# A shared SBUF area moved from an odd multiple of 64 bytes to a multiple of 128, in a two-layer hybrid decoder trunk

## The chip, the cores and the metric

The kernel runs on one core of a Trainium2 chip. Its time is the device time of one execution in microseconds (us). Before the change it was 2750.69 us, the median of 3 runs (2748.47 to 2755.46).

## What is computed

The reference applies two decoder layers and a final RMSNorm to x of 1024 tokens by 1024 features, all in float32:

```
h = rmsnorm(x, norm_mix);  z = h @ w_in          # 1024 x 3336
y_ret  = retention(rq, rk, rv, rg)               # 6 heads of 64, chunks of 128 tokens
y_pool = pool_mix(pu)                            # trailing windows of 2, 4, 8, 16
y_ml   = mlstm(mq, mk, mv, mo, mi, mf)           # 4 heads of 96, chunks of 128 tokens
x = x + concat(y_ret, y_pool, y_ml) @ w_out
h = rmsnorm(x, norm_ffn);  gu = h @ w_gate_up    # 1024 x 5632
x = x + (silu(gu[:, :2816]) * gu[:, 2816:]) @ w_down
x = x + sigmoid(rmsnorm(x, norm_ple) @ w_ple_gate) * (p_i @ w_ple_proj)
```

## The kernel before, in words

Activations lie transposed in SBUF: features on the 128 partitions, in 8 groups (KC), and the 1024 tokens along the row, in two halves of 512.

**Three passes.** The large products are made in fp32r. Each float32 operand is split into a high part, rounded to fp32r, and a low part, the rest. A product is then high x high, low weight x high, and high weight x low activation, three matmuls of 128x512 into the same PSUM bank. `three_passes` (L1748 to L1753) issues them for the projections, the output projection, the first FFN tiles, the down projection and the gates; `product_of` (L1817 to L1830) does so for the FFN blocks. Each matmul has its own weight load. Twenty pairs of gate and up tiles per layer go through `block_products` (L1832), a scheme of seven products of half size in place of eight, of which four use sums of weights made by GpSimd (L1713). TensorE's other matmuls are float32: transposes, the chunk scores and states of the two mixers, the rotary permutation (L2034) and the centring of values (L2053).

**Order of the work.** One list, written out by `macro_schedule` (L85), is walked by each engine's program: norm, projection units, the chunk loop of the mLSTM with projection halves in between, the retention pairs with projection halves in between, the output projection, the FFN, and the per-layer embedding. Each engine waits on semaphores for what it needs.

**Who does what.** SP issues the loads of the weights in a fixed order (L1659 to L1670) into `w_raw` (two slots) and, in the FFN blocks, also into `turns`. GpSimd splits a weight tile into `w_hi` and `w_lo` (L1698, L1702), a ring of three tiles; for the FFN blocks ScalarE makes the high part (L1322) and GpSimd the low one (L1709). VectorE empties PSUM (L663, L1005), makes the low parts of activations (L560, L1012, L1077) and does most of the mixers' arithmetic. ScalarE makes the high parts of activations, the functions, and issues the DMAs of activations, which go to HBM and back between the FFN's two halves.

**Where things lie.** `build` allocates these tensors one after another, each start rounded up to 32 bytes; the numbers are bytes in a partition: `w_raw` at 1152, `w_hi` at 9344, `w_lo` at 21632, `const` at 33920, `par`, `early`, `rstd` at 45216, `turns` at 49312, `rows` at 57504, `small` at 65696, `zero1` at 65952 (4 bytes). Then comes the shared area, which `arena_at` (L272) and the allocation `arena` (L273) set, at 65984. The tensors in it are placed by hand with `at` (L276) and overlap in time. From its start: `h_hi`, `h_lo`, `x` and `mix` of 32768 bytes each, and from `w_at` 30720 bytes for what a stage needs. In `x`'s place lie `ml_qk` and `ret_qkv` for a time, in `mix`'s place `ffn_b` and `ple_in`, in `h_lo`'s `h_whole`, and behind `w_at` `ml_v`, `conv_raw`, `ml_kw`, `ml_c`, `ml_cols` (at 20032), `ml_so` (at 20672), `ml_vx`, `ml_km`, `ret_t`, `ffn_bw`, `p_hi`, `p_lo`, `ple_sig`, `squares`, `silu_g`, `square_sum`, `act`, `diag` and `w_sum`. The rows of an activation, 512 tokens of 4 bytes, begin at multiples of 2048 bytes from the area's start. `stat` and `tmp16` (L337, L338) are allocated behind it, `stat` at 227840.

```
WB = 30720
arena_at = -(-nc.sbuf_base // 64) * 64
sb("arena", [P, (4 * XB + WB + 64) // 4])
hh_at, hl_at, x_at, mix_at, w_at = [arena_at + i * XB for i in range(5)]
...
def three_passes(out, slot, col, rhi, rlo, first, final):
    wh, wl = whi[:, slot, col:col + P], wlo[:, slot, col:col + P]
    pe.matmul(out, wh, rhi, start=first, stop=False)
    pe.matmul(out, wl, rhi, start=False, stop=False)
    return pe.matmul(out, wh, rlo, start=False, stop=final)
```

Of the kernel before, what the change touches and what calls it, by code (L numbers as in the profile page):

```python
# [14 lines left out]
P = 128  # L15
# [227 lines left out]
def build(nc, w_d, x_d, p_d, pos_d, const_d, par_d, early_d, out_d):  # L243
# [3 lines left out]
    with ExitStack() as ctx:  # L247
        def sb(name, shape, dt=F32):
            return ctx.enter_context(nc.sbuf_tensor(name, shape, dt))[:]
# [19 lines left out]
        zero1 = sb("zero1", [P, 1])  # L269
        XB = 4 * KC * S  # L270
        WB = 30720
        arena_at = -(-nc.sbuf_base // 64) * 64  # L272
        sb("arena", [P, (4 * XB + WB + 64) // 4])  # L273
        hh_at, hl_at, x_at, mix_at, w_at = [arena_at + i * XB for i in range(5)]

        def at(name, offset, shape, dt=F32):  # L276
# [2026 lines left out]
```

## Time and profile before

| | |
|---|---|
| median of 3 runs | 2750.69 us |
| profiled execution | 2751.61 us |
| its span, first to last instruction | 2749.8 us |
| mean granted TensorE clock | 0.978 of full |
| TensorE busy | 2622.8 us, 95% |
| VectorE busy | 1506.1 us, 55% |
| GpSimd busy | 1284.3 us, 47% |
| ScalarE busy | 712.8 us, 26% |
| moved by DMA | 192.06 MB, 70 GB/s |

The span is divided among the engines by busy time, which overlaps from engine to engine. A matmul's duration runs until its result is out, so matmuls that follow one another overlap in the records, and their rate is read from their starts. A float32 matmul stands as two instructions in the records. A name such as h_hi<-x,par lists what is written and what is read; for a matmul the moving operand comes first and the weights second. PE, PEld, DVE, ACT and POOL are TensorE's matmuls, its weight loads, VectorE, ScalarE and GpSimd.

### The profile page before, as it was taken

To read this page: it belongs to the slowest core of one execution; us is meant where nothing else is said; L and a number is where in the kernel's file an instruction comes from. 1 tells how busy PE (TensorE), PEld (TensorE's weight loads), DVE (VectorE), ACT (ScalarE), POOL (GpSimd) and SP (SyncE) were. 2 spreads that over 40 slices of the span, in tenths; PEclk is the share of its full clock that TensorE was granted. 3 is DMA by queue.
4 is the path that set the end of the run, shared out by engine and by line. 5 is a ranking of instruction groups with operands and counts; after the bars stand their busy time and mean duration, and the time that the engine had idled before them with its cause. 6 is when DMAs were issued, how large, how long until landed. Compare 5 with 4: busy or idle time off the path is not lost.

```text
span 2749.8 us, 30657 instructions
## 1 busy us (share of the span) xinstructions
PE 2622.8 (95%) x12324; PEld 2134.9 (78%) x12324; DVE 1506.1 (55%) x1966; ACT 712.8 (26%) x1096; POOL 1284.3 (47%) x739
## 2 busy tenths in 40 slices
PE   7889998999999999999988999989999999999997
PEld 5678876878888878887776887768788888788875
DVE  6967755674333353354778577556633333424556
ACT  3020122333333340123221002142433333210132
POOL 4322221337878764443433222214488878444431
PEclk9999998999999999999999999999999999999998
DMA  3110101112232341311121000021132322422111
GB/s 141 40 43 31 46 32 69 54 54 78 83 92 70 92 184 45 112 65 46 46 102 39 31 31 31 31 77 54 62 92 69 92 77 85 161 104 73 46 47 61
DMA packets 48285, 192.06 MB, mean 70 GB/s; under 512 B 5520, under 2 KB 5776, under 8 KB 43792
## 3 DMA queue, kind: packets, MB, share of 16 engines
q1 hardware_dynamic: 32544, 116.41, 13.4%
q10 hardware_dynamic: 15600, 73.70, 6.9%
q8 instruction: 98, 1.61, 0.2%
q14 instruction: 43, 0.35, 0.0%
HBM read 157.05 MB, written 32.51 MB: 69 GB/s over the span
## 4 chain that ended last, share of the span: by engine, by line
PE 84%; DVE 12%; ACT 3%; issue 1%; DMA 0%; ACTq 0%; DVEq 0%
PE proj L1751 16%; PE proj L1753 16%; PE proj L1752 16%; PE proj L1829 5%; PE proj L1827 5%; PE proj L1828 5%; PE aux L1829 5%; PE aux L1827 5%; PE aux L1828 5%; DVE ml_qk L678 2%; DVE mix L689 1%; PE aux L1976 1%; DVE mix L687 1%; PE aux L2008 1%; PE aux L1997 1%
## 5 line engine op out<-in xcount | busy, mean ns | idle before, releaser
L1698 POOL TENSOR_TENSOR w_hi<-w_raw,zero 128x1024 fp32r<-128x1024 f32 (+1 forms) x145 | 271.3, 1871 | 1210.3 <-PE proj L1753 1196.4
L1751 PE MATMUL proj<-h_hi,w_hi 128*128 128x512 f32 x1792 | 722.5, 403 | 52.9 <-DVE conv_raw L663 21.3
L1753 PE MATMUL proj<-h_lo,w_hi 128*128 128x512 f32 x1792 | 709.2, 396 | 0.0
L1752 PE MATMUL proj<-h_hi,w_lo 128*128 128x512 f32 x1792 | 706.2, 394 | 0.0
L1751 PEld LDWEIGHTS proj<-h_hi,w_hi 128*128 128x128 f32 x1792 | 341.6, 191 | 135.2 <-issue 55.0
L1752 PEld LDWEIGHTS proj<-h_hi,w_lo 128*128 128x128 f32 x1792 | 341.7, 191 | 76.1 <-issue 2.6
L1753 PEld LDWEIGHTS proj<-h_lo,w_hi 128*128 128x128 f32 x1792 | 341.0, 190 | 76.4
L1702 POOL TENSOR_TENSOR w_lo<-w_raw,w_hi 128x1024 fp32r<-128x1024 f32 (+1 forms) x145 | 389.8, 2688 | 11.4
L1005 DVE TENSOR_TENSOR x<-x,proj 128x512 f32<-128x512 f32 x128 | 87.8, 687 | 333.8 <-PE proj L1753 333.8
L1709 POOL TENSOR_TENSOR w_lo<-w_raw,w_hi 128x512 fp32r<-128x512 f32 x120 | 183.9, 1534 | 109.5 <-ACT w_hi L1322 109.5
L1709 POOL TENSOR_TENSOR w_lo<-turns,w_hi 128x512 fp32r<-128x512 f32 x120 | 181.3, 1511 | 65.0 <-ACT w_hi L1322 65.0
L1751 PE MATMUL proj<-ffn_b,w_hi 128*128 128x512 f32 x320 | 127.8, 399 | 14.3 <-DVE ffn_b L1012 12.8
L1294 ACT ACTIVATE squares<-x 128x512 f32<-128x512 f32 x96 | 60.7, 632 | 308.6 <-DVE x L1005 242.5
L1753 PE MATMUL proj<-ffn_b,w_hi 128*128 128x512 f32 x320 | 126.7, 396 | 0.0
L1752 PE MATMUL proj<-ffn_b,w_lo 128*128 128x512 f32 x320 | 125.8, 393 | 0.0
L1829 PE MATMUL aux<-h_lo,w_hi 128*128 128x512 f32 x320 | 125.8, 393 | 0.0
L1829 PE MATMUL proj<-h_lo,w_hi 128*128 128x512 f32 x320 | 125.8, 393 | 0.0
L1827 PE MATMUL proj<-h_hi,w_hi 128*128 128x512 f32 x320 | 125.1, 391 | 0.0
L1827 PE MATMUL aux<-h_hi,w_hi 128*128 128x512 f32 x320 | 125.1, 391 | 0.0
L1828 PE MATMUL proj<-h_hi,w_lo 128*128 128x512 f32 x320 | 124.8, 390 | 0.0
L1828 PE MATMUL aux<-h_hi,w_lo 128*128 128x512 f32 x320 | 124.8, 390 | 0.0
L1322 ACT ACTIVATE w_hi<-turns 128x512 fp32r<-128x512 f32 x120 | 75.6, 630 | 142.1 <-PE proj L1829 102.0
(285 smaller groups left out, 4506.4 us busy)
## 6 DMA issues: line engine op xcount, KB each, us to landing
w_raw<-weights SPq DMA_DIRECT2D x170, 512.0 KB, 3.2
act_spill<-act ACTq DMA_DIRECT2D x44, 512.0 KB, 5.1
turns<-weights SPq DMA_DIRECT2D x40, 512.0 KB, 4.1
h_whole<-act_spill ACTq DMA_DIRECT2D x12, 1024.0 KB, 8.8
ffn_b_whole<-act_spill ACTq DMA_DIRECT2D x8, 1024.0 KB, 5.9
w_raw<-weights SPq DMA_DIRECT2D x16, 384.0 KB, 3.0
x<-x_in ACTq DMA_DIRECT2D x8, 512.0 KB, 8.5
x_spill<-x ACTq DMA_DIRECT2D x1, 4096.0 KB, 11.6
```

The costliest lines, as they stand in the source:

```text
L1005: v.tensor_tensor(x[:, m, hs(h)], x[:, m, hs(h)], pbank(u, k), ALU.add).then_inc(emptied[bank(u, k)].sem, 1)
L1294: a.activation(sqr[:, j % 2, :], x[:, c, hs(h)], ACT.Square).then_inc(sq_made.sem, 1)
L1322: a.activation(operand_slot(L, b, i)[0], block_weights(L, b)[i], ACT.Copy).then_inc(operand_hi.sem, 1)
L1698: g.tensor_tensor(whi[:, slot, 0:n], w, zero1[:, 0:1].to_broadcast([P, n]), ALU.add).then_inc(w_hi_made, 1)
L1702: g.tensor_tensor(wlo[:, slot, 0:n], w, whi[:, slot, 0:n].bitcast(F32), ALU.subtract).then_inc(weights_ready.sem, 1)
L1709: g.tensor_tensor(lo, block_weights(L, b)[i], hi.bitcast(F32), ALU.subtract).then_inc(operand_ready.sem, 1)
L1751: pe.matmul(out, wh, rhi, start=first, stop=False)
L1752: pe.matmul(out, wl, rhi, start=False, stop=False)
L1753: return pe.matmul(out, wh, rlo, start=False, stop=final)
L1827: pe.matmul(out, wh[:, o], hi, start=first and j == 0, stop=False, skip_group_check=True)
L1828: pe.matmul(out, wl[:, o], hi, start=False, stop=False, skip_group_check=True)
L1829: ins = pe.matmul(out, wh[:, o], lo, start=False, stop=j == 3, skip_group_check=True)
```

## The change

The start of the area is rounded up to a multiple of 128 bytes in place of 64, and the area's allocation is made 64 bytes longer so that it still holds everything. The area's start goes from 65984 to 66048, and with it everything in it; `stat` goes from 227840 to 227904, `tmp16` by as much. Nothing else changes.

```diff
         XB = 4 * KC * S
         WB = 30720
-        arena_at = -(-nc.sbuf_base // 64) * 64
-        sb("arena", [P, (4 * XB + WB + 64) // 4])
+        arena_at = -(-nc.sbuf_base // 128) * 128
+        sb("arena", [P, (4 * XB + WB + 128) // 4])
         hh_at, hl_at, x_at, mix_at, w_at = [arena_at + i * XB for i in range(5)]
```

## Rows read from the trace of the kernel before

**Rows 1.** The page: span, busy time by engine, granted clock in 40 slices.

```profile
span 2749.8 us, 30657 instructions
PE 2622.8 (95%) x12324; PEld 2134.9 (78%) x12324; DVE 1506.1 (55%) x1966; ACT 712.8 (26%) x1096; POOL 1284.3 (47%) x739
...
PEclk9999998999999999999999999999999999999998
```

**Rows 2.** The chain that ended last: by engine (page), by line (the chain in full).

```profile
PE 84%; DVE 12%; ACT 3%; issue 1%; DMA 0%; ACTq 0%; DVEq 0%
...
by line: PE proj L1751 16.4%; PE proj L1753 16.2%; PE proj L1752 16.0%; PE proj L1829 4.7%; PE proj L1827 4.7%; PE proj L1828 4.6%; PE aux L1829 4.6%; PE aux L1827 4.5%; PE aux L1828 4.5%; DVE ml_qk L678 2.0%; issue 1.1%; DVE mix L689 1.0%;
```

**Rows 3.** Busy time by stretch: engine, us, instructions; clock, DMA share, GB/s.

```profile
60.00:175.00 115.00, 99.67 (x437) 80.82 (x435) 96.43 (x100) 13.48 (x19) 41.84 (x18) 0.94 0.13 42
175.00:345.00 170.00, 165.37 (x935) 142.56 (x936) 130.49 (x278) 20.34 (x27) 42.04 (x19) 0.98 0.11 38
...
500.00:587.00 87.00, 86.10 (x374) 69.58 (x372) 65.60 (x64) 24.89 (x41) 38.03 (x17) 0.98 0.13 43
650.00:1000.00 350.00, 350.00 (x1530) 287.16 (x1530) 128.81 (x162) 127.11 (x217) 279.71 (x199) 1.00 0.28 88
1050.00:1250.00 200.00, 200.00 (x876) 164.09 (x875) 83.10 (x77) 23.69 (x32) 89.80 (x42) 1.00 0.21 74
```

**Rows 4.** TensorE in order of time, FFN blocks: start us, duration us.

```profile
699.95 0.39 PE L1827 MATMUL proj<-ffn_b,w_hi 128*128 128x512 f32 x1
700.18 0.39 PE L1828 MATMUL proj<-ffn_b,w_lo 128*128 128x512 f32 x1
...
702.92 0.39 PE L1828 MATMUL proj<-ffn_b,w_lo 128*128 128x512 f32 x1
```

**Rows 5.** TensorE in order of time, after a pause, at the lower clock.

```profile
1016.08 0.63 PE L1752 MATMUL proj<-ffn_b,w_lo 128*128 128x512 f32 x1
1016.51 0.63 PE L1753 MATMUL proj<-ffn_b,w_hi 128*128 128x512 f32 x1
...
1017.79 0.63 PE L1753 MATMUL proj<-ffn_b,w_hi 128*128 128x512 f32 x1
```

**Rows 6.** The chain in order of time: a float32 product of 128x512.

```profile
350.40 3.43 PE aux L2034 x8
```

**Rows 7.** Groups by line and shape, POOL, ACT and DVE: busy us, mean ns.

```profile
L1713 POOL TENSOR_TENSOR w_sum<-turns 128x512 f32<-128x512 f32 x20 | 25.8, 1292 | 0.0
L1713 POOL TENSOR_TENSOR w_sum<-w_raw 128x512 f32<-128x512 f32 x20 | 25.8, 1290 | 0.0
...
L1322 ACT ACTIVATE w_hi<-turns 128x512 fp32r<-128x512 f32 x120 | 75.6, 630 | 142.1 <-PE proj L1829 102.0 <-POOL turns L1713 40.0
L1322 ACT ACTIVATE w_hi<-w_raw 128x512 fp32r<-128x512 f32 x120 | 75.0, 629 | 143.0 <-PE aux L1829 95.6 <-POOL w_raw L1713 47.4
L1322 ACT ACTIVATE w_hi<-w_sum 128x512 fp32r<-128x512 f32 x40 | 24.6, 616 | 0.0
...
L1005 DVE TENSOR_TENSOR x<-x,proj 128x512 f32<-128x512 f32 x128 | 87.8, 687 | 333.8 <-PE proj L1753 333.8
L1111 DVE TENSOR_TENSOR silu_g<-proj,rstd 128x512 f32<-128x512 f32 x20 | 13.8, 691 | 18.8 <-PE proj L1829 18.8
...
L854 DVE TENSOR_REDUCE stat<-ml_tmp 128x4 f32<-128x384 f32 x16 | 8.9, 554 | 0.6
L846 DVE TENSOR_REDUCE small<-ml_v 128x4 f32<-128x384 f32 x16 | 8.8, 553 | 0.6
```

**Rows 8.** The chain in order of time: short float32 matmuls.

```profile
360.21 1.79 PE aux L2053 x16
...
241.71 1.34 PE aux L1997 x12
```

**Rows 9.** DMA issues on the page: KB each, us to landing.

```profile
x<-x_in ACTq DMA_DIRECT2D x8, 512.0 KB, 8.5
```

## The prediction, made before the changed kernel was run

> **What bounds the kernel now.** I read the page first: TensorE is busy 95% of the span, and the granted clock stands at the full level nearly everywhere [rows 1]. Then the chain of waits: 84% of it is TensorE, and DMA is no part of it [rows 2]. The nine entries of the three-pass products (L1751 to L1753, L1827 to L1829) add up to 16.4 + 16.2 + 16.0 + 4.7 + 4.7 + 4.6 + 4.6 + 4.5 + 4.5 = 76.2%, or 2095 us of 2749.8. So the time is set by how fast 128x512 fp32r matmuls follow one another, and the reader should look at that spacing, not at the 390 to 400 ns that a listing gives for one of them (they overlap).
>
> The busy times by stretch give the spacing [rows 3]: in the middle of the FFN blocks TensorE starts 1530 matmuls in 350.00 us without a gap, 228.8 ns each; in the down projection 876 in 200.00 us, 228.3 ns (a stretch also counts one or two that reach over its edges). The order of time shows the same, 13 steps from 699.95 to 702.92 us, 228.5 ns each [rows 4]. Where the clock has fallen to its lower level of 1.2 GHz, four steps take 1.71 us, 427 ns each [rows 5]: 512 columns at 1.2 GHz are 426.7 ns, with nothing on top. At 2.4 GHz the same columns are 213.3 ns, so a matmul at the full clock pays 15.5 ns that it doesn't pay at half of it. The fp32 matmuls of L2034 read as many bytes at half that rate: eight instructions in 3.43 us, 428.8 ns each, 2.0 ns over the columns, at the full clock [rows 6]. So some 2 ns are a step's own cost, and 13.4 ns are left that appear only where the moving operand is drawn at 4 bytes per 2.4 GHz cycle.
>
> **What the change moves.** The tensors ahead of the area are rounded up to 32 bytes each, and by their shapes it begins at byte 65,984 = 515 x 128 + 64. After the change it begins at 66,048 = 516 x 128. The change does take effect, then: every moving operand of the three passes (h_hi, h_lo, ffn_b, ffn_bw, p_hi, p_lo) lies in the area at a multiple of 2048 bytes from its start, so all of them go from 64 past a 128-byte boundary to on it. No instruction, wait or DMA is added, removed or reordered. The weights (w_hi, w_lo) stay on 128-byte boundaries.
>
> **TensorE's moving reads.** The surplus has a size that the address would give. A row of 2048 bytes that begins 64 past a boundary touches 17 pieces of 128 bytes, an aligned one 16. If such pieces are drawn at the speed of the full clock, 17 of them take 213.3 x 17/16 = 226.7 ns, and with the 2.0 ns of [rows 6] a step is 228.7 ns: the measured 228.8. At half the clock, and for fp32 at half the rate, 226.7 ns of drawing hide behind 426.7 ns of columns, and no surplus should show; none does [rows 5, 6]. I know no other reading that meets all three figures without a number of its own. Aligned, a step is then 213.3 + 2.0 = 215.3 ns, 13.4 ns less. The trace has no fp32r matmul from another alignment, so the bounds are: at best the whole surplus goes (15.5 ns), at worst none; I take 13.4, the nearest in mechanism. [...]
>
> The sum: 2095 us of chain less some 60 us in which the clock is low or a product starts up (a mean clock of 0.978 over two levels is 4.4% of the span at the lower one, much of it in stages with few products) leave 2035 us, 8,900 steps of 228.8 ns. 8,900 x 13.4 ns = 119 us.
>
> **What takes over.** In the FFN blocks POOL is next: 279.7 us busy of 350 [rows 3], 80%; with 350 shrunk by 5.9% to 329.5 us it is 85%, and TensorE still has no gap. In the gate and convolution stage (60 to 175 us, and again in the second layer) DVE is busy 96.4 of 115 us [rows 3], its steps are on the chain themselves, and only the products' own share shrinks, which the sum has counted. Where products set the pace in the mLSTM loop and the output projection, DVE is busy 130.5 of 170 us and 65.6 of 87 [rows 3], so it has about a quarter to spare. Products that end just ahead of a DVE result bring nothing; I take 4 us off for them. That leaves 115 us.
>
> **DVE, ScalarE, GpSimd.** They read and write the area too, and their times don't follow the address [rows 7]: GpSimd writes w_sum (in the area) from turns (32 past a boundary) in 1292 ns and from w_raw (on a boundary) in 1290; ScalarE makes w_hi from turns in 630, from w_raw in 629, from w_sum in 616 ns; DVE adds a fill to x, 64 past, in 687 ns, and takes a fill by rstd, 32 past, in 691. I cost these at nothing. The bound is 1% of DVE's 12% of the chain, 3 us either way. Three small things go the other way, onto odd multiples of 64: ml_cols, ml_so and stat. stat is written by L854 in 554 ns, and small, 32 past, by L846 in 553 [rows 7]: nothing.
>
> **Weight loads.** Where a short matmul is paced by its weight load, a step is 1.79/16 = 112 ns (L2053, weights 64 past, moving operand on a boundary) and 1.34/12 = 112 ns (L1997, weights and the moving ml_c both from tensors 64 past) [rows 8]. Those stay, which is why only the fp32r steps are in the sum.
>
> **DMA.** The inputs of x land 8.5 us after issue [rows 9]; the chain has 0% of DMA [rows 2] beside the first 6 us. Whether an aligned end is faster lies between 0 and 2 us for those 6; I take 0.
>
> **The sum.** The profiled execution took 2751.6 us (span 2749.8), 0.9 above the median of the runs. 2751.6 − 115 = 2636.6, and by the median 2636.
>
> **The rivals.** *The surplus belongs to the change of weights.* Every fp32r matmul here has a weight load of its own beside it, also fp32, and 13.4 ns could be the hand-over between two streams at full rate. For it: the trace has not one fp32r matmul without it, and no aligned one, so the two can't be told apart by a row; and L2053 and L1997 show weight loads, not addresses, as the pace [rows 8]. Against it: a hand-over would have to vanish at half clock and for fp32, where the weight is changed as well [rows 5, 6], and would hit 17/16 by accident. The time is then unchanged, 2751, within 3 us. [...]
>
> *Only part of it is the address*: the piece is 64 bytes in truth and the rest of the surplus something else, so that a step drops by about 6.7 ns; 8,900 x 6.7 = 60 us, 2692.
>
> *Slower: the two streams of TensorE collide.* Weights now lie on a 128-byte boundary and moving rows half a piece beside them; after the change both start alike. If that made each step wait for one more piece, 13.3 ns, it would be 8,900 x 13.3 = 118 us, 2870; it decides the result from 0.9 ns a step. Against it: L2053 and L1997, with like and unlike starts, are equal [rows 8].
>
> *Another engine takes the gain*: products are faster, but POOL in the FFN blocks or DVE in the output projection sets the end. At POOL's 80% the blocks could shrink by 20% before that, so I give it no case of its own; a fifth of the gain lost would be 2655.
>
> **How the numbers follow.** Aligned reads at full speed 0.60, in part 0.06, weight hand-over (no change) 0.28, collision 0.06. The first case's own range is 2615 (8,900 x 15.5 = 138 us) to 2655. The range must reach to the unchanged case, since the first two hold 0.66 alone: 2615 to 2757. A measurement of this kernel can tell about 0.3% (8 us) from no change. Faster by more 0.66, within 0.28, slower 0.06.
>
> **What would show it.** Right: between the FFN blocks' matmuls some 215 ns in place of 228.8, so about 1,625 in 350 us; 427 ns at the low clock and 428.8 ns at L2034 as before; DVE, ScalarE and POOL times unchanged with POOL's share near 85%; the gain spread over all product stages by their count. Wrong: a spacing of 228 to 229 ns with a span within 8 us (hand-over), or one near 242 ns (collision); or a spacing of 215 with gaps before L1827 or L1751 that POOL ends.

## The result and the profile after

The changed kernel takes 2790.6 us (median of 4 runs, 2787.65 to 2792.47) against 2753.1 us for the kernel before beside it (2748.47 to 2758.86). The ratio is 1.013, with an interval of 1.011 to 1.015: slower, where the prediction had 2636 us and faster. Of all the runs in this document one, a sixth of run 16, took 3779.5 us at a granted clock of 0.649 where its others have 0.975 to 0.981, and it is left out of run 16's figures.

The page of the changed kernel, its span, busy times, granted clock and chain by engine, to be read against [rows 1, 2]:

```profile
span 2790.7 us, 30657 instructions
PE 2659.7 (95%) x12324; PEld 2140.7 (77%) x12324; DVE 1499.4 (54%) x1966; ACT 713.6 (26%) x1096; POOL 1286.6 (46%) x739
...
PEclk9999999999999999999999999999999999999998
...
PE 85%; DVE 10%; ACT 3%; issue 1%; DMA 0%; ACTq 0%; DVEq 0%
```

The instructions are the same in number and stand in the same order on every engine. The span grew by 2790.7 − 2749.8 = 40.9 us, and TensorE's busy time by 2659.7 − 2622.8 = 36.9 us; TensorE's idle time is 131.0 us where it was 127.0. The other engines moved by less than 7 us each. So nearly all of it is time in which TensorE works.

Busy time by stretch, the changed kernel, in the columns of [rows 3], with one stretch more (650 to 950), in which the experiments below are compared:

```profile
60.00:175.00 115.00, 99.94 (x427) 80.17 (x425) 96.66 (x99) 13.48 (x19) 43.39 (x18) 0.93 0.13 42
175.00:345.00 170.00, 165.86 (x929) 142.03 (x930) 129.05 (x277) 20.35 (x27) 42.16 (x19) 0.98 0.11 37
500.00:587.00 87.00, 86.43 (x378) 69.34 (x376) 64.46 (x61) 25.14 (x42) 37.70 (x17) 1.00 0.13 43
650.00:950.00 300.00, 300.00 (x1292) 243.24 (x1291) 106.05 (x139) 107.77 (x184) 235.90 (x169) 1.00 0.27 83
650.00:1000.00 350.00, 350.00 (x1508) 283.75 (x1507) 122.99 (x162) 125.62 (x215) 277.11 (x198) 1.00 0.27 82
1050.00:1250.00 200.00, 200.00 (x859) 160.87 (x858) 80.89 (x74) 21.79 (x29) 88.04 (x40) 1.00 0.21 73
```

In the FFN blocks 1530 matmuls in 350 us have become 1508, and in the down projection 876 in 200 us have become 859, with no gap in either and the clock at 1.00. The spacing went from 228.8 to 232.1 ns and from 228.3 to 232.8 ns. TensorE in order of time shows it step by step, at the place of [rows 4]:

```profile
699.53 0.39 PE L1829 MATMUL aux<-h_lo,w_hi 128*128 128x512 f32 x1
699.75 0.39 PE L1827 MATMUL aux<-h_hi,w_hi 128*128 128x512 f32 x1
...
702.55 0.39 PE L1827 MATMUL aux<-ffn_bw,w_hi 128*128 128x512 f32 x1
```

Thirteen steps take 3.02 us, 232.3 ns each, where thirteen took 2.97 us. Between steps at the full clock the trace has a mean of 228.99 ns before and 232.53 ns after, worked out from the starts of all that have such a neighbour (9,927 and 9,940 steps of less than 250 ns). 9,940 x 3.54 ns = 35 us, of the 36.9 that TensorE is busier. The stages say the same. At the same matmul the changed kernel is 6 us behind at the start of the first layer's FFN blocks, 12 at their end, 22 in the second layer's mLSTM loop, 30 and 36 at the start and the end of the second layer's FFN blocks, and 41 at the end: it grows with the number of products.

What did not move is shown by the counterparts of [rows 5, 6, 8]. First a piece at the lower clock, TensorE in order of time:

```profile
1029.67 0.63 PE L1752 MATMUL proj<-ffn_b,w_lo 128*128 128x512 f32 x1
1030.10 0.63 PE L1753 MATMUL proj<-ffn_b,w_hi 128*128 128x512 f32 x1
...
1031.38 0.63 PE L1753 MATMUL proj<-ffn_b,w_hi 128*128 128x512 f32 x1
```

Four steps take 1.71 us, 427 ns each, to the hundredth what they took before, and the granted clock is 0.50 there in both traces (1016.05 to 1017.80 us before, 1029.60 to 1031.40 us after). The 213.3 ns that the columns are given at the full clock, here and in the prediction, are an estimate from it: 427 ns for 512 columns at half the clock are 1.2 columns a ns, and twice that is the prediction's 2.4 GHz at a column a cycle. No run measured the clock in GHz. Then the chain in order of time, the float32 products:

```profile
351.79 3.43 PE aux L2034 x8
...
361.66 1.79 PE aux L2053 x16
```

Both are those of before (3.43 and 1.79 us). The groups by line and shape of the three other engines, for [rows 7]:

```profile
L1005 DVE TENSOR_TENSOR x<-x,proj 128x512 f32<-128x512 f32 x128 | 87.7, 686 | 344.4 <-PE proj L1753 344.2
L1322 ACT ACTIVATE w_hi<-turns 128x512 fp32r<-128x512 f32 x120 | 75.6, 630 | 145.3 <-PE proj L1829 108.0 <-POOL turns L1713 37.3
L1713 POOL TENSOR_TENSOR w_sum<-turns 128x512 f32<-128x512 f32 x20 | 25.9, 1292 | 0.0
L854 DVE TENSOR_REDUCE stat<-ml_tmp 128x4 f32<-128x384 f32 x16 | 8.8, 553 | 0.6
```

Each of these stands within 1 ns of what it was. So the cost lies in one place, the step of an fp32r product at the full clock. It follows the place of the area, and the opposite way from the one that was predicted.

### The profile page after: what moved, and what is told of

The parts are those of the page before. It is cut to its first block, busy times and chain, and to the rows that moved or that the text cites. A ratio compares the mean times of both kernels' runs of the same rounds, so it can differ in the third digit from the quotient of the medians.

```text
span 2790.7 us, 30657 instructions
## 1 busy us (share of the span) xinstructions
PE 2659.7 (95%) x12324; PEld 2140.7 (77%) x12324; DVE 1499.4 (54%) x1966; ACT 713.6 (26%) x1096; POOL 1286.6 (46%) x739
## 3 DMA queue, kind: packets, MB, share of 16 engines
q1 hardware_dynamic: 32544, 116.41, 13.3%
## 4 chain that ended last, share of the span: by engine, by line
PE 85%; DVE 10%; ACT 3%; issue 1%; DMA 0%; ACTq 0%; DVEq 0%
PE proj L1751 17%; PE proj L1752 17%; PE proj L1753 17%; PE proj L1827 5%; PE proj L1829 5%; PE proj L1828 5%; PE aux L1829 5%; PE aux L1828 5%; PE aux L1827 5%; DVE ml_qk L678 2%; DVE mix L689 1%; PE aux L1976 1%; PE aux L2034 1%; DVE mix L687 1%; PE aux L2008 1%
## 5 line engine op out<-in xcount | busy, mean ns | idle before, releaser
L1751 PE MATMUL proj<-h_hi,w_hi 128*128 128x512 f32 x1792 | 726.5, 405 | 50.0 <-DVE conv_raw L663 20.6
L1752 PE MATMUL proj<-h_hi,w_lo 128*128 128x512 f32 x1792 | 713.7, 398 | 0.0
L1751 PEld LDWEIGHTS proj<-h_hi,w_hi 128*128 128x128 f32 x1792 | 342.4, 191 | 138.5 <-issue 53.4
L1709 POOL TENSOR_TENSOR w_lo<-w_raw,w_hi 128x512 fp32r<-128x512 f32 x120 | 183.8, 1533 | 127.0 <-ACT w_hi L1322 127.0
L1751 PE MATMUL proj<-ffn_b,w_hi 128*128 128x512 f32 x320 | 130.6, 408 | 15.2 <-DVE ffn_b L1012 14.1
L1828 PE MATMUL proj<-h_hi,w_lo 128*128 128x512 f32 x320 | 126.2, 394 | 0.0
L1827 PE MATMUL proj<-h_hi,w_hi 128*128 128x512 f32 x320 | 126.1, 394 | 0.0
L1827 PE MATMUL aux<-h_hi,w_hi 128*128 128x512 f32 x320 | 126.1, 394 | 0.0
## 6 DMA issues: line engine op xcount, KB each, us to landing
x_spill<-x ACTq DMA_DIRECT2D x1, 4096.0 KB, 11.7
```

The costliest lines, as they stand in the source:

```text
L1709: g.tensor_tensor(lo, block_weights(L, b)[i], hi.bitcast(F32), ALU.subtract).then_inc(operand_ready.sem, 1)
L1827: pe.matmul(out, wh[:, o], hi, start=first and j == 0, stop=False, skip_group_check=True)
L1828: pe.matmul(out, wl[:, o], hi, start=False, stop=False, skip_group_check=True)
```

## The experiments

**The theories.** The prediction looked at one address, that of the moving rows. The result leaves two kinds of explanation: the moving rows' own place counts (but with another sign or another period), or their place against that of the weights, which TensorE loads beside the running matmul (in the FFN blocks of the kernel before, each load starts 2 to 4 ns after a matmul and takes 188 ns). Before and after, w_hi and w_lo begin at 128 past a multiple of 256 bytes (their slots are multiples of 256 long), the area at 192 and at 0 past one. *Distance* below is the start of the area less the start of the weights, modulo 256: 64 before, 128 after. All kernels differ from the kernel before, not from the changed one. The code shown leaves out the lines in between. Where a line is added ahead of the products, their line numbers are one or two higher.

**Weights moved, runs 1 and 2.** Both move the weights by 64 bytes, and they differ in the area.

```
+ sb("pad_a", [P, 16])                 # ahead of w_hi
+ sb("pad_b", [P, 16])                 # behind w_lo
- arena_at = -(-nc.sbuf_base // 64) * 64
- sb("arena", [P, (4 * XB + WB + 64) // 4])
+ arena_at = 66304                     # run 1: area as after;  run 2: 66240
+ sb("arena", [P, (arena_at - nc.sbuf_base + 4 * XB + WB) // 4])
```

> The area begins on a multiple of 128 bytes (66,304, also of 256, as in the changed kernel), and the tensors w_hi and w_lo begin 64 past one. Theory R (the relative place of the weight stream and the moving stream matters; 64 apart is the better): 2751 us and a spacing of 228.8 ns in the FFN blocks, as before the change. Theory A (the moving operand's own address matters, on a boundary is the worse): 2790 us and 232.4 ns.

> The area begins 64 past a multiple of 128 (66,240, 192 past one of 256, as before the change), and w_hi and w_lo begin 64 past one as well. Theory R: both alike, so 2790 us and 232.4 ns. Theory A: 2751 us and 228.8 ns.

Run 1 took 2754.6 us (10 runs), a ratio of 1.001 with an interval of 1.000 to 1.002; run 2 took 2729.5 us (4 runs), 0.993 with 0.991 to 0.995. Busy time by stretch of run 1, then of run 2, in the columns of [rows 3]:

```profile
650.00:950.00 300.00, 300.00 (x1312) 246.15 (x1311) 112.10 (x141) 109.82 (x188) 242.69 (x174) 1.00 0.27 80
1100.00:1250.00 150.00, 150.00 (x657) 123.08 (x656) 65.77 (x62) 23.71 (x32) 66.91 (x32) 1.00 0.23 85
```

```profile
650.00:950.00 300.00, 300.00 (x1325) 248.42 (x1324) 117.40 (x144) 111.40 (x191) 242.38 (x173) 1.00 0.28 83
1100.00:1250.00 150.00, 150.00 (x663) 124.28 (x662) 68.11 (x65) 25.40 (x35) 66.71 (x31) 1.00 0.23 80
```

The same stretch of the kernel before:

```profile
650.00:950.00 300.00, 300.00 (x1312) 246.13 (x1312) 111.25 (x140) 109.97 (x188) 242.46 (x173) 1.00 0.26 82
```

The area of run 1 lies on a multiple of 256, as in the changed kernel, and yet its 1312 matmuls in 300 us are those of the kernel before (the changed kernel has 1292). With the weights moved along, the loss is gone. Run 2 has the area at 192 past, as before, and now 1325 matmuls, 226.67 ns each by their starts. One place of the area, two spacings: what counts is the place against the weights. The gates are an exception to run 1's figure: 259 matmuls in the 60 us from 1306 us, 233.33 ns each by their starts, where the kernel before has 264 and 228.9 ns. Run 1 fits theory R of the expectations and not A; run 2 fits neither, since R took both starts alike for the bad case (232.4 ns) and A had 228.8.

**Weights left, area moved, runs 3 to 5.**

```
- arena_at = -(-nc.sbuf_base // 64) * 64
- sb("arena", [P, (4 * XB + WB + 64) // 4])
+ arena_at = 66016                     # run 3;  run 4: 66112;  run 5: 66176
+ sb("arena", [P, (arena_at - nc.sbuf_base + 4 * XB + WB) // 4])
```

> Only the area moves, to 66,016, 96 past a multiple of 128, weights on a boundary. Theory R has no figure for 96 yet; if the two streams want to be as far apart as possible, between 228.8 and 232.4 ns, some 2770 us. Theory A, if being on a 64-byte boundary matters at all: 232.4 ns or more, over 2790 us.

> Only the area moves, to 66,112: 64 past a multiple of 128, as before, but 64 and not 192 past one of 256. Theories R and A with a period of 128 bytes: 228.8 ns and 2751 us, the same as before. If the period is 256 bytes, another figure.

> Only the area moves, to 66,176: 128 past a multiple of 256, as w_hi and w_lo are. Theory D (what counts is the distance of the moving rows' start from the weights' start, modulo 256 bytes; so far 0 gives 226.7 ns, 64 gives 228.9, 96 and 192 give 233.3, 128 gives 232.4 to 233.3): distance 0, so 226.7 ns and 2730 us. Theory S (each stream's own place modulo 256 counts, and run 2 was fast because both streams lay 192 past): the weights are at 128 as before, so not 226.7 but 228.9 ns or more, 2750 us or more.

Run 3 (distance 96) took 2795.9 us, a ratio of 1.016 (1.013 to 1.018). Run 4 (192) took 2796.6 us, 1.016 (1.014 to 1.018). Run 5 (0) took 2737.6 us, the median of 6 runs from 2728.5 to 2746.6, 0.995 (0.994 to 0.997). Busy time by stretch of runs 3, 4 and 5:

```profile
650.00:950.00 300.00, 300.00 (x1287) 241.38 (x1286) 104.62 (x138) 108.37 (x184) 235.60 (x169) 1.00 0.26 81
```

```profile
650.00:950.00 300.00, 300.00 (x1287) 241.71 (x1286) 102.81 (x137) 108.39 (x185) 237.03 (x171) 1.00 0.26 81
```

```profile
span 2726.7 us, 30657 instructions
PE 2601.0 (95%) x12324; PEld 2134.0 (78%) x12324; DVE 1509.3 (55%) x1966; ACT 713.2 (26%) x1096; POOL 1283.3 (47%) x739
...
650.00:950.00 300.00, 300.00 (x1325) 248.39 (x1324) 115.39 (x143) 110.78 (x190) 241.50 (x174) 1.00 0.28 85
1100.00:1250.00 150.00, 150.00 (x664) 124.24 (x663) 69.37 (x65) 26.07 (x38) 68.53 (x32) 1.00 0.21 75
```

Run 3 came out slower than R had it (some 2770 us), and run 4 is not the 2751 us that both theories had for a period of 128. Run 4 settles that the parity of 64 is not what matters. Its area is on an odd multiple of 64, as before, and it is as slow as run 3. Run 5 is on an even one, as after, and it is the fast one: a distance of 0, with 1325 in 300 us, as in run 2. Theory D said so, and theory S, with 228.9 ns or more, falls. Its profiled execution ends 23.1 us earlier than the kernel before, of which 21.8 are TensorE's busy time (2622.8 to 2601.0). By the starts the mean step is 226.93 ns, 2.06 below before: 9,930 x 2.06 = 20.5 us. The gain is spread as the loss was: 2 us at the start of the mLSTM loop, 6 at the start of the first FFN blocks, 10 at their end, 20 at the end of the second ones.

**The period, runs 6 to 8.** The edit is that of run 3, with the area at 66,208, 66,144 and 66,432.

> Only the area moves, to 66,208, a distance of 32 from the weights modulo 256. Theory D with a smooth dependence: between 226.7 (0) and 228.9 ns (64), 2730 to 2750 us. If only whole multiples of 64 are good, 233.3 ns as at 96, 2795 us.

> Only the area moves, to 66,144, 32 bytes ahead of the weights modulo 256 (distance 224). Theory D, if sign doesn't matter: the same as run 6. If the moving rows must start at or behind the weights: 233.3 ns, 2795 us.

> The area moves to 66,432: distance 0 modulo 256 as in run 5, but 256 and not 0 modulo 512. Theory D with a period of 256 bytes: 226.7 ns and 2730 us. A period of 512 or more: another figure, 228.9 ns or above.

One run each: 2788.7 us (distance 32), 2793.9 us (224) and 2728.4 us (0, and a multiple of 256 further on than run 5). Busy time by stretch of the three:

```profile
650.00:950.00 300.00, 300.00 (x1287) 240.95 (x1286) 101.63 (x136) 107.97 (x183) 237.02 (x170) 1.00 0.26 83
```

```profile
650.00:950.00 300.00, 300.00 (x1287) 241.58 (x1286) 104.07 (x138) 108.31 (x185) 235.57 (x168) 1.00 0.26 84
```

```profile
650.00:950.00 300.00, 300.00 (x1325) 248.39 (x1325) 115.13 (x143) 110.76 (x189) 241.44 (x173) 1.00 0.27 85
```

A shift of 256 bytes changes nothing (run 8 is run 5), and one of 128 does (after against run 5), so the period is 256. A distance of 32 in either direction already costs the whole 6.7 ns, so the smooth dependence of theory D falls. The dip is narrow (226.67 ns at 0, 233.33 at 32 and at 224), and of the seven distances tried 64 is the only other one that is cheap, at 228.89 ns; 64 in the other direction, 192 (run 4), is not. A distance of 160 was not tried.

**One weights tensor moved, runs 11 and 12.** w_hi feeds the first and the third pass, w_lo the second. A pad between them puts them 128 apart.

```
  whi = sb("w_hi", [P, RING, 1024], F32R)
+ sb("pad_a", [P, 32])
  wlo = sb("w_lo", [P, RING, 1024], F32R)
+ arena_at = 66304                     # run 11: equal to w_lo;  run 12: 66432, equal to w_hi
```

> w_lo is moved by 128 bytes and the area begins at 66,304: distance 128 to w_hi, 0 to w_lo. The load of w_lo runs beside one matmul of three, the loads of w_hi beside the other two. Theory B (what counts for a matmul is the distance to the load beside it): one step of three as at distance 0 (226.7 ns) and two as at 128 (232.4 to 233.3), mean 230.5 to 231.1 ns, 2770 us. If the worst of the two tensors sets it for all: 232.4 ns or more, 2790 us.

> The mirror: w_lo moved by 128 bytes, the area at 66,432, distance 0 to w_hi and 128 to w_lo. Theory B: two steps of three at 226.7 and one at 232.4 to 233.3, mean 228.6 to 228.9 ns, 2750 us. Worst of two: 232.4 ns or more, 2790 us.

Run 11 took 2788.7 us and run 12 2777.9 us, one run each. The kernel before, run once beside runs 9 to 12, took 2768.2 us, 15 to 20 us above its other medians at the same clock, so here only the spacings are compared. Busy time by stretch of each, and then TensorE of run 12 in order of time:

```profile
650.00:950.00 300.00, 300.00 (x1288) 241.45 (x1287) 102.29 (x136) 108.23 (x183) 236.94 (x170) 1.00 0.27 83
```

```profile
650.00:950.00 300.00, 300.00 (x1300) 245.56 (x1299) 106.56 (x139) 108.26 (x185) 236.99 (x171) 1.00 0.28 85
```

```profile
701.63 0.40 PE L1828 MATMUL aux<-ffn_bw,w_hi 128*128 128x512 f32 x1
701.86 0.40 PE L1829 MATMUL aux<-ffn_bw,w_lo 128*128 128x512 f32 x1
702.10 0.39 PE L1830 MATMUL aux<-ffn_bw,w_hi 128*128 128x512 f32 x1
702.32 0.40 PE L1828 MATMUL aux<-ffn_bw,w_hi 128*128 128x512 f32 x1
```

With w_lo alone at distance 0 nothing is gained: 233.33 ns on the mean, as in run 3. With w_hi alone at 0 the mean is 231.11 ns. From one start to the next in run 12, the first pass takes 232.5 ns, the second 234.1 and the third 226.7 in the FFN blocks (701.63, 701.86, 702.10 and 702.32 us above), and within 1.5 ns of that in the other stretches. Each load starts 2 to 4 ns after the matmul that it runs beside: in the first pass it is the load for the second (w_lo, at 128), in the second and the third one of w_hi. So one step in three has the fast 226.7 ns, and not two as a price for each step by its own weights would have it. The theory that the expectations call B, with 228.6 to 228.9 ns for run 12 and 230.5 to 231.1 for run 11, is wrong to that extent; that the worse of the two tensors sets all steps fits run 11 and not run 12. The second pass is slow although the load beside it is at distance 0. In run 11 the first is (232.4 ns), although the load beside it is w_lo's, at 0. Both come behind a step whose load is at 128. It looks, then, as if such a load holds up more than the step that it lies beside; this is read from the two runs and was not tested by itself.

**Shorter loads, runs 9, 10 and 13 to 15.** If a step waits for a share of the load that collides with it, fewer weight columns should make it shorter. In the gate products behind the down projection (the units from U_GATE on, eight in a layer; all others stay) the load is cut to 64, then 32 of its 128 columns.

```
- wh, wl = whi[:, slot, col:col + P], wlo[:, slot, col:col + P]
+ n = out.shape[0]
+ wh, wl = whi[:, slot, col:col + n], wlo[:, slot, col:col + n]
...
+ to = pbank(u, h)[0:64] if u >= U_GATE else pbank(u, h)     # 0:32 in runs 13 to 15
```

The kernel so leaves out half, then three quarters, of the gate values, and the matmul has that much fewer output rows: the edit shortens the load and narrows the product at once.

> The changed kernel, whose gate products (L1767 to L1773 for the last eight units of a layer) use 64 of the 128 weight columns; the other half of the gates is left out. Everything else keeps full loads and is the control, at 232.4 to 233.3 ns. Theory L (the surplus over 213.3 ns is made by the weight load that runs beside a matmul, column by column): the gate matmuls fall to about 213.3 + 20.0/2 = 223 ns, the rest stays. Theory M (the surplus is the moving stream's own, and the load only shifts its phase): 232 ns in the gates too.

> The same edit with the area at distance 0 from the weights (66,176), control 226.7 ns. Theory L: the gate matmuls fall to about 213.3 + 13.3/2 = 220 ns. Theory M: 226.7 ns.

> As run 9, with 32 of 128 weight columns in the gate products (three quarters of the gates left out), area at distance 128. Theory L (the surplus is made by the load beside the matmul): the gate matmuls come down to 213.3 ns plus a rest of a few ns, below 220, and the same in runs 13, 14 and 15. Theory M (the moving stream has a surplus of its own by its address): at least two of the three differ, the aligned ones below the one that lies 64 past a boundary by up to 13 ns.

> The same at distance 0 (area at 66,176, on a multiple of 128). Theory L: the same figure as run 13, below 220 ns. Theory M: as run 13 but unlike run 15.

> The same at distance 64 (area at 65,984 as before the change, 64 past a multiple of 128). Theory L: the same figure as runs 13 and 14. Theory M: up to 13 ns more than those.

The loads did get shorter. Groups by line and shape in a stretch of those gates, run 9 and then run 13 (busy us, mean ns of one load; a full one takes 188 to 191):

```profile
L1754 PEld LDWEIGHTS proj<-h_lo,w_hi 128*64 128x64 f32 x22 | 3.0, 134 | 2.1
```

```profile
L1753 PEld LDWEIGHTS proj<-h_hi,w_lo 128*32 128x32 f32 x22 | 2.4, 108 | 2.7
```

The steps did not shrink in proportion. Busy time by stretch in the gates of runs 9, 10, 13, 14 and 15:

```profile
1306.00:1366.00 60.00, 60.00 (x263) 35.18 (x262) 39.94 (x38) 12.36 (x20) 25.59 (x12) 1.00 0.16 49
1282.00:1342.00 60.00, 60.00 (x263) 34.99 (x262) 41.39 (x40) 12.81 (x21) 23.72 (x11) 1.00 0.14 47
1306.00:1366.00 60.00, 60.00 (x262) 28.16 (x261) 39.17 (x37) 12.46 (x20) 26.04 (x12) 1.00 0.14 46
1306.00:1366.00 60.00, 60.00 (x260) 28.21 (x259) 45.91 (x46) 14.17 (x23) 24.17 (x11) 1.00 0.17 53
1306.00:1366.00 60.00, 60.00 (x261) 28.06 (x260) 45.13 (x43) 13.29 (x21) 26.65 (x12) 1.00 0.13 44
```

By their starts, with 64 columns they are 229.3 ns at distance 128 and 230.0 ns at distance 0; with 32 columns 230.7 ns at 128, 231.7 at 0 and 231.1 at 64. (Full loads in the same kernels: 232.4 at 128, 226.7 at 0, 228.9 at 64.) With the shorter load at most 1.0 ns of the dependence on the distance is left, with the other sign, but a step stays 16 to 18 ns above the estimated 213.3 ns of its columns, and above the 226.67 ns of the best step with a full load. The whole kernels, one run each, took 2791.1 us (run 9), 2739.0 (10), 2793.0 (13), 2739.3 (14) and 2756.6 (15). The theories L and M of the expectations both fall. That the dependence went with the full load fits a clash of two streams; the size of what is left fits nothing that I have.

**Two-byte values, runs 17 and 18.** In the same gates all four operands are read as the upper two bytes of each value, in steps of four bytes, so that a column is as wide in SBUF but half as much is taken. Area at 66,048 and 66,176.

```
+ if narrow_type:                      # u >= U_GATE
+     wh, wl, rhi, rlo = [t.bitcast(mybir.dt.bfloat16)[:, 1::2] for t in (wh, wl, rhi, rlo)]
```

> The changed kernel's places (distance 128). The gate products read h and the weights as bf16, the upper half of each 4-byte value, over the same bytes in steps of 4; the gates so lose precision. Control stages at 232.4 to 233.3 ns. Theory W (the surplus and its dependence on the distance come with 4-byte operands, which use the full width of the reads): the gate matmuls come to 213.3 + about 2 = 215 to 216 ns. Theory H (a hand-over between matmuls that every stream pays): 226 ns or more here too.

> The same at distance 0. Theory W: again 215 to 216 ns in the gates, and no difference from run 17. If it is the bytes spanned and not the bytes read that count: as the controls, 226.7 ns here and 232.4 to 233.3 in run 17.

Busy time by stretch, in the gates, run 17 and then run 18:

```profile
1306.00:1366.00 60.00, 60.00 (x268) 25.81 (x267) 38.74 (x37) 13.74 (x21) 27.27 (x12) 1.00 0.14 45
```

```profile
1282.00:1342.00 60.00, 60.00 (x268) 25.63 (x267) 42.86 (x41) 13.26 (x21) 25.13 (x12) 1.00 0.13 45
```

268 steps in 60 us in both, 225.3 and 225.0 ns by their starts: with two-byte values the distance makes 0.3 ns. The other products of the same two kernels show 233.33 and 226.67 ns. The whole kernels took 2789.7 and 2735.7 us, one run each. Theory W is right that the dependence goes, but not that the step falls to 215 to 216 ns; 12 ns over the columns stay, close to what theory H had (226 or more). How wide the reads are, which W takes as its ground, no run shows.

What took the dependence away is not settled by this, because the weight load changed too. Groups by line and shape, run 17:

```profile
L1754 PEld LDWEIGHTS proj<-h_hi,w_lo 128*128 128x128 bf16 x256 | 24.8, 97 | 32.6
```

A two-byte load of 128 columns takes 97 ns (run 18: 96) where a four-byte one takes 188 to 191, and with four-byte values a shorter load alone had left little of the dependence (runs 9, 10 and 13 to 15). It may be the bytes or the length of the load. Both operands were narrowed together; one alone was not tried. What is shown is that the dependence appears with four-byte operands and a full load at the full clock, and with less than that is at most 1.0 ns in the cases tried.

**A third pair at distance 0, run 16.** The weights are moved to a multiple of 256 and the area is put on one.

```
+ sb("pad_a", [P, 32])                 # ahead of w_hi
+ arena_at = 66304
```

> w_hi and w_lo move by 128 bytes onto multiples of 256, and the area begins at 66,304, also a multiple of 256, as in the changed kernel; full loads. Theory D (distance modulo 256): 226.7 ns in all stages and 2728 to 2738 us, as in runs 2, 5 and 8. If the area's place at a multiple of 256 were itself the bad one: 232.4 ns and 2790 us.

It took 2730.5 us (median of 5 runs), a ratio of 0.993 (0.991 to 0.995). Busy time by stretch:

```profile
650.00:950.00 300.00, 300.00 (x1325) 248.41 (x1324) 115.03 (x142) 111.14 (x190) 242.00 (x174) 1.00 0.27 85
```

Its area is on a multiple of 256, as in the changed kernel: the place that the change aimed at is fast once the weights are there as well.

**All placements with both weights tensors alike.** Places are modulo 256. The spacing is that of the down projection, worked out from the starts between 1100 and 1250 us. The times are medians of 4 to 10 runs; runs 6, 7 and 8 have one each.

| kernel | weights | area | distance | spacing, ns | time, us |
|---|---|---|---|---|---|
| before | 128 | 192 | 64 | 228.89 | 2753.1 |
| after | 128 | 0 | 128 | 233.33 | 2790.6 |
| run 1 | 192 | 0 | 64 | 228.89 | 2754.6 |
| run 2 | 192 | 192 | 0 | 226.67 | 2729.5 |
| run 3 | 128 | 224 | 96 | 233.33 | 2795.9 |
| run 4 | 128 | 64 | 192 | 233.33 | 2796.6 |
| run 5 | 128 | 128 | 0 | 226.67 | 2737.6 |
| run 6 | 128 | 160 | 32 | 233.33 | 2788.7 |
| run 7 | 128 | 96 | 224 | 233.33 | 2793.9 |
| run 8 | 128 | 128 | 0 | 226.67 | 2728.4 |
| run 16 | 0 | 0 | 0 | 226.67 | 2730.5 |

Three pairs of absolute places at distance 0 give one spacing in this stage, 226.67 ns, and two at 64 give one, 228.89 ns. Against the kernel before, runs 2, 5 and 16 are each faster by 0.5 to 0.7%, so all three beat both kernels. Run 5 is the one to keep: it is the change's own two lines with another place. Its runs spread over 18 us; the profiled one, with a mean clock of 0.979, is the fastest of them.

## Why the prediction was wrong

**The bound: right.** The nine entries of the chain (76.2% before) are 77.7% of it after. The spacing of the fp32r matmuls sets the time, and the kernels in the table stand in three groups by it: 2728 to 2738 us, 2753 to 2755, and 2789 to 2797.

**What the change moves: right.** All moving operands of the three passes went along, and no instruction moved. The term "8,900 steps" was 10% low, 9,900 in the trace: it was taken from the chain's share, and what the chain gives to products is no count of them (it rose by 73 us where the span rose by 41, and DVE's part fell from 12 to 10%).

**The step that failed is "TensorE's moving reads".** It took the surplus for the price of 17 pieces of 128 bytes in place of 16, and with it −13.4 ns a step and −119 us. Measured: +3.5 ns a step and +35 us. A step of 215.3 ns exists nowhere in these runs; the best of an fp32r product is 226.67 ns. No run shows a piece of 128 bytes: the piece and its size were the author's estimate. The theory asked for a minimum wherever the area is on a multiple of 128. After, run 1 and run 16 are all on a multiple of 256, and show 233.33, 228.89 and 226.67 ns. A real spacing has the value of 213.3 x 17/16, 226.7 ns, but at distance 0, with the area at 0, at 128 and at 192 past a multiple of 256 alike, so an extra piece at an odd start is not where it comes from; what makes it is open. The text said "I know no other reading that meets all three figures without a number of its own", and that was the weak point. Three figures met by one free choice (the size of the piece) carry less than they seem to, when all of them come from one placement.

**The weights were left out of the address.** The prediction noted that they "stay on 128-byte boundaries" and went on. Its part on weight loads looked at them only where a short product waits for one, and there it was right (L2053 and L1997 did not move); the fp32r steps were left out of it. This was the other half of the mechanism: the place of two tensors changed against each other, and only one of them was watched.

**The rivals.** *The two streams of TensorE collide* had the sign and the mechanism, at a chance of 0.06. Its size was off: 13.3 ns a step was assumed (one more piece), 3.5 were measured in the mean and 4.4 in the down projection, so 2790.6 us and not 2870. The reason against it, that L2053 and L1997 show like and unlike starts equal, doesn't hold. These are float32 products, which L2034 shows at half the rate (428.8 ns for 512 columns), and take 112 ns with 128 moving columns (L2053) and with 97 (L1997), so the columns don't pace them; they are no case of two streams at the rate of the fp32r steps; L2053's 1.79 us stand unchanged after. The same text used the half rate to explain why no surplus shows at L2034, and should have applied it here. It had also set both starts alike as the bad case: the runs show alike as the best, and the changed kernel as 128 apart modulo 256, which "on a 128-byte boundary" hides. *The hand-over* (no change) is part of the truth. A surplus of at least 11.7 ns over the estimated 213.3 stays at every placement tried, in two-byte products too (225.0 ns in run 18), so it isn't the distance; what it is stays open. *Only part of it is the address* is right in words, with the other sign for this change. *Another engine takes the gain* had nothing to take.

The sign could not have been read from the trace of before, since it has one placement. But the range could have been wider: no row excluded that the surplus grows, and L2053 and L1997 were weak evidence against it. The upper end was put at no change all the same.

**What takes over: right as far as it was asked.** No gap opened ahead of L1827 or L1751, and POOL's busy time in the FFN blocks' stretch is 277.1 of 350 us, 79%. The wait that grew most is small. Waits of TensorE, the changed kernel (us in total, times, longest):

```profile
PE proj L1751 <- DVE conv_raw L663: 20.6, 4, 9.7
PE proj L1751 <- DVE h_lo L603: 17.5, 5, 12.6
PE aux L1880 <- DVE diag L552: 10.8, 2, 5.4
```

The first was 21.3 and the second 18.6 us; the last was 3.4 us, so it grew by 7.4. With others that shrank, the idle time of TensorE grew by 4 us of the span's 40.9.

**DVE, ScalarE, GpSimd, DMA: right.** The rows under the result stand within 1 ns of before. The largest move among [rows 7] is ScalarE's w_hi from w_sum, 616 to 624 ns, 40 times: 0.3 us, and off the chain. The bound of 3 us either way was not used. The 0 taken for the moved stat was right as well (L854 takes 553 ns).

## What to carry to other kernels

Where fp32r matmuls at the full clock are the bound and each has a weight load of its own, try the moving tensors and the weights at the same place modulo 256 bytes. In this kernel a step then took 226.67 ns where it took 228.89 at a distance of 64 and 232.4 to 233.33 at the others tried; that is worth 0.5 to 0.7% against the distance of 64 and some 2% against the others. One tensor put on a rounder number by itself can lose: here 1.3%. When the trace has a single placement, a fine numerical fit of a stall is one point; the range should hold both signs.

## What the runs showed of the hardware

- The weight load and the moving stream of TensorE are not free of each other. An fp32r 128x512 step with a full load takes 226.67 ns at distance 0 (runs 2, 5, 8 and 16), 228.89 at 64 (the kernel before and run 1, but for the gates of run 1 with 233.33), 232.4 to 233.3 at 128 (the changed kernel) and 233.33 at 32, 96, 192 and 224 (runs 6, 3, 4 and 7). The loads themselves take 187 to 188 ns in the FFN blocks at every distance (192 for one of three in run 12), so it is the matmuls that give way. With four-byte operands the step depends on where the two lie against each other; with two-byte operands and loads of 97 and 96 ns it doesn't (225.3 ns at 128 in run 17, 225.0 at 0 in run 18).
- With four-byte operands and full loads the steps come in a grid. Three steps take 680.0 ns at distance 0, 686.7 at 64, 693.3 in run 12 and 700.0 in run 3, each 6.67 ns apart, which is the time of 16 columns if 512 take the estimated 213.3 ns. (In time order the steps of run 3 read 231, 231 or 232, and 237 or 238 ns, over and over, those of run 5 226 and 227.) The changed kernel's FFN blocks have a cycle of seven steps, 1626.6 ns. The distance alone does not decide between such patterns, nor does the stage: at the same distance of 128 the down projection of runs 9 and 13 has 232.4 ns, and the FFN blocks of run 17 have 233.33; at 64 the gates of run 1 have 233.33 and those of the kernel before 228.9. Why there are two was not tried.
- Where the granted clock is 0.50 the step is 427 ns in each of the four kernels read for it (84 steps before, 89 after, 86 in run 5, 87 in run 3). At the full clock no stage of products came below 225 ns on the mean (run 18's gates), for an estimated 213.3 ns of columns. A matmul without a load of its own was not tried, and neither were distances finer than 32 bytes and that of 160.
- A load of 64 columns took 134 ns and one of 32 108 ns (runs 9 and 13), but the step beside them was 229 to 232 ns. What paces it then stays open.
